# Two projection stages, with the inner k steps issued as pairs of 64-row products on the two halves of the array

## The reference, cut to what matters

```
# first mixer, h = rmsnorm(x, norm_a)
z = h @ w_in                       # its last 1024 columns are the gate
...
return o.reshape(b, s, BRANCH_WIDTH) * jax.nn.silu(gate)
# second mixer's output
x = x + y @ w_out_b[idx]
```

## Time and profile before

| | |
|---|---|
| time, median of 3 runs | 3396.63 us (3396.53 to 3397.31) |
| span of the profiled execution | 3395.0 us |
| PE busy | 3295.9 us, 97% of the span |
| PEld busy | 2842.4 us, 84% |
| DVE, ACT, POOL busy | 2052.7, 1642.6, 1395.5 us |
| PE records | 18165 |

### The profile page before, as it was taken

One profiled execution on the slowest core, in us unless ns is written; L12 is line 12 of the kernel. 1 busy time (PEld: TensorE's weight loads), 2 busy tenths in 40 slices (PEclk: granted clock), 3 DMA queues, 4 the chain that ended last, 5 costly groups with the idle time before them and its releaser, 6 DMA issues. The chain is left out here.

```text
span 3395.0 us, 56731 instructions
## 1 busy us (share of the span) xinstructions
PE 3295.9 (97%) x18165; PEld 2842.4 (84%) x18165; DVE 2052.7 (60%) x4209; ACT 1642.6 (48%) x3846; POOL 1395.5 (41%) x1778
## 2 busy tenths in 40 slices
PE   8999999999999989999999999999999899999999
PEld 7887788999999988778998878888787778888787
DVE  7456773444666667547887566565347766565335
ACT  3566216557566761426665643333244743333333
POOL 6564544555667865213334334443002244443000
PEclk9999999999999999999999999999999899999999
DMA  8211772111222126300001222222464122222464
GB/s 306 71 32 46 285 280 82 45 35 55 64 61 65 60 67 257 114 1 25 0 0 37 107 79 82 76 90 81 145 221 149 50 75 92 75 86 87 141 199 161
DMA packets 111984, 338.26 MB, mean 100 GB/s; under 512 B 11793, under 2 KB 40385, under 8 KB 102978
## 3 DMA queue, kind: packets, MB, share of 16 engines
q1 hardware_dynamic: 111810, 336.12, 28.3%
HBM read 274.18 MB, written 61.10 MB: 99 GB/s over the span
## 5 line engine op out<-in xcount | busy, mean ns | idle before, releaser
L2184 PE MATMUL ps<-down_high,hidden_high 128*128 128x512 f32 x688 | 269.2, 391 | 7.1 <-DVE hidden_low L2051 4.3
L2185 PE MATMUL ps<-down_low,hidden_high 128*128 128x512 f32 x688 | 268.0, 390 | 0.0
L2186 PE MATMUL ps<-down_high,hidden_low 128*128 128x512 f32 x688 | 268.0, 389 | 0.0
L2120 PE MATMUL ps<-columns_combined,up_high_even 128*128 128x512 f32 (+1 forms) x648 | 248.7, 384 | 11.0 <-DVE columns_combined L4230 2.7
L2049 DVE TENSOR_TENSOR down_low<-down_raw,down_high 128x1024 fp32r<-128x1024 f32 x86 | 108.6, 1263 | 247.5 <-ACT down_high L1962 247.4
L2121 PE MATMUL ps<-columns_combined,up_high_even 128*128 128x512 f32 (+1 forms) x648 | 247.6, 382 | 0.0
L2122 PE MATMUL ps<-columns_combined,up_low_even 128*128 128x512 f32 (+1 forms) x648 | 247.5, 382 | 0.0
L2120 PE MATMUL ps<-columns_combined,up_high_odd 128*128 128x512 f32 x616 | 240.3, 390 | 4.4 <-DVE gates L2057 4.4
L2121 PE MATMUL ps<-columns_combined,up_high_odd 128*128 128x512 f32 x616 | 240.4, 390 | 0.0
L2122 PE MATMUL ps<-columns_combined,up_low_odd 128*128 128x512 f32 x616 | 240.3, 390 | 0.0
L1148 ACT ACTIVATE masked_then_probs<-masked_then_probs,unit_rows 128x256 f32<-128x256 f32 (+1 forms) x512 | 229.0, 450 | 22.2 <-DVE sink_term L1236 20.8
(11 more groups left out here) (473 smaller groups left out, 9892.9 us busy)
## 6 DMA issues: line engine op xcount, KB each, us to landing
mod_weights<-in_w_mod SPq DMA_DIRECT2D x48, 1024.0 KB, 6.3
up_raw<-in_w_up SPq DMA_DIRECT2D x44, 1024.0 KB, 4.8
down_raw<-in_w_down SPq DMA_DIRECT2D x88, 512.0 KB, 3.6
hidden_columns<-hidden SPq DMA_DIRECT2D x44, 512.0 KB, 2.6
hidden_columns<-hidden_columns SPq DMA_DIRECT2D x88, 256.0 KB, 3.9
w_unit_raw<-in_w_in_b SPq DMA_DIRECT2D x22, 768.0 KB, 4.4
x_kept<-x SPq DMA_DIRECT2D x24, 512.0 KB, 2.8
group_rows<-unit_rows SPq DMA_DIRECT2D x64, 132.0 KB, 1.8
```

What stands on the lines that cost most here:

```text
L2120: nc.tensor.matmul(out, a_hi, z_hi, start=(start and k == 0 and first == 0), stop=False, **again)
L2184: nc.tensor.matmul(out, h_hi[to][:, t], down_hi[to][:, cols], start=begin, stop=False)
L2185: nc.tensor.matmul(out, h_hi[to][:, t], down_lo[to][:, cols], start=False, stop=False)
L2186: last = nc.tensor.matmul(out, h_lo[to][:, t], down_hi[to][:, cols], start=False, stop=(end and to == self.slot(h, f, s)))
```

## The change

The steps k = 1 to 6 of both stages no longer issue three full products per tile. A new function, `beside`, takes two tiles at a time: for position m it issues the products of rows 0 to 63 for tile m (the lower half) and those of rows 64 to 127 for tile (m + 4) mod 8 (the upper half), alternately. Over the eight positions each tile gets both halves once, so a step has 48 products of 64 rows where it had 24 of 128. The two halves of one tile go to the same bank four positions apart, and a new semaphore, `halves`, makes the second wait until the first is done (and likewise from one step to the next). Steps 0 and 7 are as before.

```
+def beside(nc, lower, upper):
+    for n, (x, w) in enumerate(((0, 0), (0, 1), (1, 0))):
+        for half, (out, first, xs, ws) in ((slice(0, P // 2), lower), (slice(P // 2, P), upper)):
+            last = nc.tensor.matmul(out, xs[x][half], ws[w][half], start=(first and n == 0), stop=False, skip_group_check=True)
+    return last
...
+                        if 0 < k < KT - 1:
+                            crossed = 7 * ((KT - 2) * c + k - 1)
+                            for m in range(TILES):
+                                if m >= 4:
+                                    pe.wait_ge(core.halves.sem, core.halves.at(crossed + m - 3))
+                                elif k > 1 and m < 3:
+                                    pe.wait_ge(core.halves.sem, core.halves.at(crossed + m - 2))
+                                elif k > 1:
+                                    pe.wait_ge(core.split_used.sem, core.split_used.at((KT - 1) * c + k))
+                                lower, upper = ((core.ps[:, i, :], False, (plain_tokens(t_hi, k, i), plain_tokens(t_lo, k, i)),
+                                                 (weights.hi[:, s], weights.lo[:, s])) for i in (m, (m + 4) % TILES))
+                                done = core.halves if m < TILES - 1 else core.split_used
+                                beside(core.nc, lower, upper).then_inc(done.sem, 1)
+                            continue
```

More of the change, by code:

```diff
@@ L206, in __init__ @@
         self.gate_stored = Count(nc, ctx, "gate_stored")
+        self.halves = Count(nc, ctx, "halves")
     def mark(self):
@@ L399, in _ @@
                                 context.turn(pe, t, ps[:, 2 * t:2 * t + 2, :])
+                        if 0 < k < KT - 1:
[7 more added lines that the diff above has]
+                                    pe.wait_ge(core.split_used.sem, core.split_used.at((KT - 1) * c + k))
+                                lower, upper = ((ps[:, i, :], False, (plain_tokens(t_hi, k, i), plain_tokens(t_lo, k, i)),
+                                                 (weights.hi[:, s], weights.lo[:, s])) for i in (m, (m + 4) % TILES))
+                                done = core.halves if m < TILES - 1 else core.split_used
+                                beside(nc, lower, upper).then_inc(done.sem, 1)
+                            continue
                         for m in (range(TILES) if k or c == 0 else (4, 5, 6, 7, 0, 1, 2, 3)):
@@ L416, in mixer_out @@
     for c, n in ((core.raw0, 16 * CHUNKS), (core.raw1, 16 * CHUNKS), (core.split, KT * CHUNKS), (core.high, KT * CHUNKS), (core.ready2, 16),
-                 (core.split_used, (KT - 1) * CHUNKS), (core.acc, TILES * CHUNKS), (core.acc_used_dve, TILES * CHUNKS), (core.hi_done, KT),
+                 (core.split_used, (KT - 1) * CHUNKS), (core.halves, 7 * (KT - 2) * CHUNKS), (core.acc, TILES * CHUNKS), (core.acc_used_dve, TILES * CHUNKS), (core.hi_done, KT),
                  (core.lo_done, KT)):
@@ L2882, in opening @@
                  (core.row_vectors, 16), (core.gate_stored, 16 * TILES * CHUNKS), (core.high, KT * CHUNKS), (core.split, KT * CHUNKS),
-                 (core.split_used, (KT - 1) * CHUNKS), (core.acc, TILES * CHUNKS), (core.acc_used_act, TILES * CHUNKS), (core.sq, TILES),
+                 (core.split_used, (KT - 1) * CHUNKS), (core.halves, 7 * (KT - 2) * CHUNKS), (core.acc, TILES * CHUNKS), (core.acc_used_act, TILES * CHUNKS), (core.sq, TILES),
                  (core.links_pool, 1), (core.values, 1), (core.rstd, 1), (core.hi_done, KT), (core.lo_done, KT), (core.expo, 2), (core.beside0, 32)):
```

## The result

| | before | after |
|---|---|---|
| median of 20 runs | 3396.39 us | 3400.07 us |
| range of the runs | 3394.30 to 3399.01 | 3398.35 to 3406.13 |
| span of the profiled execution | 3395.0 us | 3399.4 us |

The ratio is 1.0012 with a 95% interval of 1.0006 to 1.0017. The change costs 3.7 us (2.0 to 5.8) where 2.9 us less were forecast. It is a small loss, but the sign is not in doubt.

A forecast was written before the change was run, and what follows sets the result against it. PE, busy 97% of the span, was taken as the bound: number of products times their 0.2267 us distance. Opening 1.2 us plus second mixer's output 1.7 us gave 2.9 us less, 3393.7 us; 80% range 3391.5 to 3406.

The forecast's parts named there:

- Two products do run side by side when each has half of the rows, and nearly no fixed part shows: Both stages' pairs: halves overlap, so a pair takes 218 ns instead of a full product's 226.7 ns.
- fixed part: The 12.7 ns of each 226.7 ns product that do not depend on its columns; at most 7.3 us to win.
- The scores' 0.215 us: Distance between pairs of 64-row products in the scores, plain float32 with 256 columns, taken as nearest evidence for the pair.
- 144 pairs x 8.7 ns = 1.25 us per chunk: Gain in each chunk of both stages from pairs at 218 ns, before the cost of changing form.
- The excursion: Going from full products to halves and back, once per chunk: 0.3 us lost, bounds 0.3 and 0.4.
- The waits: The 176 new waits between a tile's halves: taken at nothing, bounds nothing to 3.2 us.
- The cap at POOL's w_lo: Opening's chunk 1: weights ready at 55.55 us let PE arrive only 0.23 us earlier, losing 0.72 us of chunk 0's gain.
- The output's 0.2 us: Second mixer's output: loss as PE, coming earlier, waits for DVE's adds or ACT's context rows; bounds 0 and 0.95.
- Paid once per pair, started one after the other: Rival for the pairs: 226.7 ns plus some 5 ns each, 4.1 us more, 3400.7 us; chance 0.18.
- Each half pays by itself: Rival for the pairs: each half pays the 12.7 ns, 239.4 ns a pair, 8.5 us more, 3405.1 us; chance 0.15.
- no overlap: Rival for the pairs: halves run in turn, 453.4 ns a pair, 131.8 us more, 3528.4 us; chance 0.05.

The follow-up runs named there:

- y2: The changed kernel with the opening's steps 1 to 6 as full plain float32 products in 256-column pieces, second mixer's output as before: 3582.91 us, before 3396.45.
- x3: The changed kernel with every wait kept but full products issued instead of halves: 3397.18 us, -0.2 against before.
- x2: The changed kernel with halves in the second mixer's output alone, opening as before: 3400.54 us, +3.2 against before.
- z3: Halves in both chunks of the second mixer's output alone, with 8 instead of 10 DVE modulation products before the adds: 3397.60 us, +1.3 against before.
- z4: The kernel before, without halves, with 8 instead of 10 DVE modulation products before the adds: 3393.47 us, -2.8; timed again 3392.87 us, ratio 0.9988.
- z1: The changed kernel with halves only in chunk 0 of the second mixer's output, none in the opening: 3398.21 us, +1.9 against before.
- y3: The changed kernel with the opening's pairs as plain float32 in 256-column pieces, second mixer's output as before: 3583.10 us, before 3396.45.
- x1: The changed kernel with halves in the opening alone, second mixer's output as before: 3398.22 us, +0.9 against before.
- y1: The changed kernel with only the lower 64 rows' products in the opening's steps 1 to 6, second mixer's output as before: 3396.75 us, before 3396.45.

## Why the prediction was wrong, by its own steps

**"Two products do run side by side when each has half of the rows, and nearly no fixed part shows": the second half of this sentence is the step that failed.** The scores' 0.215 us was put down to the pairing, and it is the operand type: y2 shows it without any pair. The prediction named the difference of type as "what keeps this from being proof" and took 218 ns all the same. The pair took 226.7 ns, so the term of 144 pairs x 8.7 ns = 1.25 us per chunk is zero. What came out right was the first half: they overlap. A pair takes the 226.7 ns of a full product, so what lies beside the 214.0 ns is paid once per pair.

**The excursion was right in kind and too small.** 0.49 us was measured for 0.3, beyond its bounds of 0.3 to 0.4. The reading from the scores took three slow distances of 0.10 us. The rows after show two crossings and, behind each, a slow stretch of 0.155 us; the one behind the return was not in the sum. These two steps turn the forecast gain into a loss: with no gain per pair even 0.3 us per excursion gives 1.2 us more, not 2.9 less.

**The waits** were taken at nothing, and x3 gives -0.2 us of 3397 with an interval of 3 us to either side. Its steps of 5.440 us and the absence of any wait for `halves` in its trace and in after's say the same more sharply.

**The cap at POOL's w_lo** is real (five profiles wait there, 0.28 to 2 us), but it did not apply in after, where PE's first product came 1.16 us later than in the profile before and its products no faster. **The output's 0.2 us** had the place right and the sign of PE's move wrong: PE is not ahead there. With that the sum by the prediction's own form is 0 + 1.98 us, 3398.4 against the median before. That is at the near end of the measured 2.0 to 5.8 us.

**The rest, about 1.7 us, is open.** The interval of the measurement begins at 2.0 us, so it may be as good as nothing, but x2 has a rest of 2.2 us and z3 against z4 one of 3.1. Two places were found that cost single executions over 2 us. The edge of the second mixer's output is 2.3 us longer than the mean of the unchanged ones in x2 and 2.6 us in z1, their excursions taken off. But after's own two profiles have 14.97 and 14.61 us there, hardly more than before's, y2 and y3 have the late edge without halves in the stage, and z3's loss stays with the edge mended. The wait in the last feed-forward, with the clock behind it, was longer in five of eight profiles with halves and in none of ten without, which would be some 1.5 us on the average. Against both stands that the profiled executions that show them were mostly slower than their medians: 3402.26 us for 3398.21 in z1, where it was the slowest of eleven, and 3400.43 for 3398.22 in x1. No run set either place apart from chance.

**The rivals.** *Paid once per pair, started one after the other* (3400.7, 0.18) came nearest in time, and was right that the fixed part is paid once. Its own term was not there, though: the halves start 3 to 4 ns apart, but the pairs are not further apart for it (226.7 ns). That it came within 1 us is luck: its 576 x 5 ns = 2.9 us stood in for the excursions' missing 0.8 us and for the rest. The Trainium skill (TensorE: Matmul & The Clock Gate, Part 3) gives about 4 ns for each further tile. The start of the halves agrees with it; in an unbroken row of pairs this trace shows no such cost, 5.440 us for 24 as before. The Trainium skill (TensorEngine Tiling (Array Packing), The Problem) names contractions of 64 or less as what leaves the full array underused. That a contraction of 128 gained nothing from being cut, 226.7 ns for 226.7, agrees with it. *Each half pays by itself* and *no overlap* fall with the 226.7 ns.

## What to carry to other kernels

A contraction of 128 rows has nothing to win from being cut into two halves: the halves overlap, but a pair costs exactly what the full product did, and going there and back costs 0.49 us. When a duration is borrowed from another operation, the operand type must agree before anything else is read from it; one full product of that type, as in y2, would have shown it. A stretch that looks like the missing part in one profile has to be looked for in every kernel, those without the change too, before it is put down to the change. And moving two of DVE's products behind the adds, at a hand-over with a slack of 0.4 us, gave 2.8 and 4.2 us in two sets (the interval of the first still holds 1), about what this whole change had been forecast to give.

## What the runs showed of the hardware beyond that

- At the full clock, `fp32r` products of 512 columns are 226.7 ns apart whether they have 128 rows, 64 rows alone or 64 rows beside 64 others.
- Plain float32 takes two records per product, 0.215 us each for 256 columns: 0.86 us for a 128 x 512 product against 0.227 in `fp32r`. Here 288 such products cost (3582.91 - 3396.45) / 288 = 0.65 us more each. Cut into halves they take just as long.
- A change between full and half products costs 0.092 us and slows the next products by 0.155 us in all, in either direction. y1, where the halves have no partner, has the same 5.595 us in its first step of halves, so the cost comes with the 64 rows and not with the pairing.
- DVE's modulation product takes 1.22 us in one place and 2.3 us in another, with POOL operations beside it that are stretched as well.
- In the last feed-forward a PE wait of 1.18 to 1.71 us left the clock at 2.4 GHz (13 of 18 traces). After waits of 1.89 to 2.31 us (the other five) it was at 1.2 GHz for 3.4 us; that is the 0.83 granted over 10 us above. Two profiles of one kernel, x1, had 2.15 and 1.31 us.
